# A mixture-of-experts encoder layer: the gather of all sorted tokens is issued behind the first pair's gate/up products instead of the second's

## The reference

```python
g_idx = argmax(g_logits)                       # 1 group of 4
top_w, top_i = lax.top_k(e_prob, TOP_K)        # 2 experts of its 8
for e in range(N_EXPERTS):                     # 32
    hg, hu = jnp.split(t @ w_gate_up[e], 2, axis=-1)
    out = out + comb[:, e:e + 1] * ((jax.nn.silu(hg) * hu) @ w_down[e])
x = layer_norm(DEEPNORM_ALPHA * x + out)
```

## Time and profile before

| | |
|---|---|
| Median of 3 runs | 496.63 us (495.29 to 497.02) |
| Profiled execution, its span | 494.7 us |
| Profiled execution, its own time | not given beside the span |
| PE busy / PEld busy | 472.1 us (95%) / 334.4 us (68%) |
| DVE, ACT, POOL busy | 244.9, 202.1, 222.8 us |
| DMA moved | 145.13 MB, mean 293 GB/s |

### The profile page before, as it was taken

The page is one execution under the profiler, slowest core; times in us unless marked ns, Lnnn a source line. Parts: engine busy times, 40 slices in busy tenths (PEclk is TensorE's granted clock), DMA queues, the critical chain, the costliest instruction groups (busy, mean ns, idle before and its releaser), DMA issues.

```text
span 494.7 us, 7686 instructions
## 1 busy us (share of the span) xinstructions
PE 472.1 (95%) x2816; PEld 334.4 (68%) x2816; DVE 244.9 (50%) x536; ACT 202.1 (41%) x447; POOL 222.8 (45%) x187
## 2 busy tenths in 40 slices
PE   8999999999999999999998999999999999998992
PEld 6999999898999999988973544444444444343441
DVE  1089999769996445630688242222222222122116
ACT  3544554489865696454542232222212212022112
POOL 3898999756765779998308011111111111011002
PEclk9999999999999999999998999999999999898997
DMA  8799985533533445559908979999999999999932
GB/s 289 256 364 346 362 295 171 197 103 128 172 127 129 141 159 171 177 181 380 422 32 318 390 291 425 421 421 421 421 421 422 420 420 423 421 421 421 420 154 86
DMA packets 26370, 145.13 MB, mean 293 GB/s; under 512 B 3040, under 2 KB 3296, under 8 KB 13792
## 3 DMA queue, kind: packets, MB, share of 16 engines
q1 hardware_dynamic: 26336, 144.67, 74.9%
HBM read 143.61 MB, written 1.05 MB: 292 GB/s over the span
## 4 chain that ended last, share of the span: by engine, by line
PE 86%; DVE 5%; ACT 3%; issue 2%; DMA 2%; SPq 1%; POOL 1%; DVEq 0%; ACTq 0%
PE bank L1474 21%; PE bank L1507 13%; PE bank L1226 12%; PE bank L1228 12%; PE bank L1227 12%; PE bank L1522 3%; PE bank L1523 3%; DMA raw<-in_w_in 2%; PE bank L1304 1%; PE bank L1282 1%; PE bank L1496 1%; DVE info L1113 1%; POOL w_lo L478 1%; PE bank L1448 1%; PE bank L1449 1%
## 5 line engine op out<-in xcount | busy, mean ns | idle before, releaser
L478 POOL TENSOR_TENSOR w_lo<-raw,w_hi 128x512 fp32r<-128x512 f32 x140 | 182.7, 1325 | 47.3 <-ACT w_hi L543 44.5
L543 ACT CAST w_hi<-raw 128x512 fp32r<-128x512 f32 x140 | 85.0, 619 | 80.7 <-PE bank L1228 71.1
L1226 PE MATMUL bank<-x_hi,w_hi 128*128 128x256 f32 x400 | 115.6, 289 | 1.4 <-POOL w_lo L478 1.4
L1228 PE MATMUL bank<-x_hi,w_lo 128*128 128x256 f32 x400 | 113.3, 283 | 0.0
L1227 PE MATMUL bank<-x_lo,w_hi 128*128 128x256 f32 x400 | 113.3, 283 | 0.0
L1474 PE MATMUL bank<-slots,raw 128*64 128x512 f32 x368 | 112.7, 593 | 0.0
L789 DVE SCALAR_TENSOR_TENSOR bank<-slots,par,bank 128x256 f32<-128x256 f32 x232 | 92.3, 482 | 0.2
L504 POOL COPY raw<-gates 128x512 f32 x28 | 19.8, 707 | 159.1 <-PE bank L1474 138.9
L1226 PEld LDWEIGHTS bank<-x_hi,w_hi 128*128 128x128 f32 x400 | 76.7, 192 | 2.1 <-issue 1.3
L1227 PEld LDWEIGHTS bank<-x_lo,w_hi 128*128 128x128 f32 x400 | 76.8, 192 | 0.3
L1228 PEld LDWEIGHTS bank<-x_hi,w_lo 128*128 128x128 f32 x400 | 76.8, 192 | 0.0
(11 more groups left out here) (211 smaller groups left out, 638.8 us busy)
## 6 DMA issues: line engine op xcount, KB each, us to landing
slots<-in_w_gate_up SPq DMA_DIRECT2D x46, 1024.0 KB, 15.6
slots<-in_w_down SPq DMA_DIRECT2D x32, 1024.0 KB, 16.4
raw<-in_w_in SPq DMA_DIRECT2D x48, 512.0 KB, 3.6
spare<-in_w_gate_up SPq DMA_DIRECT2D x10, 1024.0 KB, 16.1
late<-in_w_gate_up SPq DMA_DIRECT2D x8, 1024.0 KB, 20.0
raw<-in_w_attn SPq DMA_DIRECT2D x8, 512.0 KB, 3.2
raw<-in_w_conv SPq DMA_DIRECT2D x8, 512.0 KB, 3.2
raw<-in_w_out SPq DMA_DIRECT2D x8, 512.0 KB, 3.3
```

Of the source, the lines that this page charges most:

```text
L478: nc.gpsimd.tensor_tensor(w_lo[:, n % SPLIT, m], raw[:, b % RAW, m], w_hi[:, n % SPLIT, m].bitcast(F32), ALU.subtract).then_inc(w_lo_done, 1)
L543: nc.scalar.copy(w_hi[:, n % SPLIT, m], raw[:, b % RAW, m]).then_inc(w_hi_done, 1)
L1226: mm(dst, ah, bh, start=first, stop=False, **kw)
L1228: return mm(dst, al, bh, start=False, stop=last, **kw)
```

## The change

`gather_sorted` is called once, before the loop over the pairs and behind `gate_up(0, 0)` and `slot_info(0, 0)`, instead of in pair 1 behind its gate/up products. The chunks are taken in the order 4 to 7, 0 to 3. ScalarE and VectorE do `copy_sorted` in pair 0 instead of pair 1, behind `swish` and gate times up. Their wait for `pads_set` becomes a wait for `x1_set` ahead of the first chunk that lies over `ln_rows`. GpSimd clears the padding only when all chunks are copied. TensorE waits for `first_copied` ahead of the gather, and no longer for all copies behind it.

```diff
--- before.py
+++ after.py
@@ -108,6 +108,9 @@
 def last_tenant(e):
 
     return max((n for n in range(e) if GU_HOME[n] == GU_HOME[e]), default=None)
+
+
+SORTED_ORDER = [4, 5, 6, 7, 0, 1, 2, 3]
 
 
 C_IDENT, C_TRI, C_IOTA = 0, P, 2 * P
@@ -495,6 +498,8 @@
                 pool.wait_ge(x1_set, t + 1)
                 nc.gpsimd.tensor_tensor(xt[:, t, :], xt[:, t, :], ln_rows[:, 1, :], ALU.add).then_inc(x1_set, 1)
             pool.wait_ge(x1_set, 2 * TT)
+            pool.wait_ge(xgT_even, KT // 2)
+            pool.wait_ge(xgT_odd, KT // 2)
             nc.gpsimd.memset(xgT[:, :, ROUTED:], 0.0).then_inc(pads_set, 1)
 
             def take_tokens(u, first, second):
@@ -506,8 +511,6 @@
 
 
             pool.wait_ge(pads_set, 1)
-            pool.wait_ge(xgT_even, KT // 2)
-            pool.wait_ge(xgT_odd, KT // 2)
             with pool.Fori(1, PAIRS // 2) as i:
                 for u in range(2):
 
@@ -706,19 +709,20 @@
                     nc.scalar.copy(y_hi[:, c * HALF:(c + 1) * HALF], y_bank[c][:]).then_inc(y_hi_done, 1)
 
             def copy_sorted():
-                act.wait_ge(pads_set, 1)
-                for k in range(0, KT, 2):
-                    act.wait_ge(gathered, k + 1)
+                for i, k in enumerate(SORTED_ORDER[0::2]):
+                    if k == 0:
+                        act.wait_ge(x1_set, 2 * TT)
+                    act.wait_ge(gathered, 2 * i + 1)
                     nc.scalar.activation(xgT[:, k, 0:ROUTED], out_bank[k % 4][:], ACT.Identity, scale=ln1_gain(k),
                                          bias=ln1_shift(k)).then_inc(xgT_even, 1)
-                    if k >= 4:
-
-                        act.wait_ge(xgT_even, k // 2 + 1)
+                    if i >= 2:
+
+                        act.wait_ge(xgT_even, i + 1)
                         nc.scalar.mul(out_bank[k % 4][:], xt[:, k % 4 // 2, 0:HALF], ALPHA).then_inc(sums_by_act, 1)
 
             def pair(p, u, last=False):
                 swish(p)
-                if is_pair(p, 1):
+                if is_pair(p, 0):
                     copy_sorted()
                 copy_hT(p)
                 if not last:
@@ -1153,20 +1157,21 @@
                                             ALU.subtract).then_inc(y_lo_done, 1)
 
             def copy_sorted():
-                dve.wait_ge(pads_set, 1)
-                for k in range(1, KT, 2):
-                    dve.wait_ge(gathered, k + 1)
+                for i, k in enumerate(SORTED_ORDER[1::2]):
+                    if k == 1:
+                        dve.wait_ge(x1_set, 2 * TT)
+                    dve.wait_ge(gathered, 2 * i + 2)
                     nc.vector.tensor_scalar(xgT[:, k, 0:ROUTED], out_bank[k % 4][:], ln1_gain(k), ln1_shift(k),
                                             ALU.mult, ALU.add).then_inc(xgT_odd, 1)
-                    if k >= 4:
-
-                        dve.wait_ge(xgT_odd, k // 2 + 1)
+                    if i >= 2:
+
+                        dve.wait_ge(xgT_odd, i + 1)
                         nc.vector.tensor_scalar(out_bank[k % 4][:], xt[:, k % 4 // 2, HALF:], ALPHA, None,
                                                 ALU.mult).then_inc(sums_by_dve, 1)
 
             def pair(p, u, build=True):
                 gate_times_up(p, u)
-                if is_pair(p, 1):
+                if is_pair(p, 0):
                     copy_sorted()
                 build_scatter(p, u)
                 if build:
@@ -1439,10 +1444,11 @@
             def gather_sorted():
 
                 pe.wait_ge(compact_built, TT)
-                for k in range(KT):
-                    if k >= 4:
-
-                        pe.wait_ge(xgT_odd if k % 2 else xgT_even, (k - 4) // 2 + 1)
+                pe.wait_ge(first_copied, KT // 2)
+                for i, k in enumerate(SORTED_ORDER):
+                    if i >= 4:
+
+                        pe.wait_ge(xgT_odd if k % 2 else xgT_even, (i - 4) // 2 + 1)
                     n = slice(k * P, (k + 1) * P)
                     for t in range(TT):
                         mm(out_bank[k % 4][:], x1_hi[:, t, n], compact[:, t, :], start=(t == 0), stop=False)
@@ -1531,11 +1537,6 @@
 
                 if p >= 1:
                     gate_up(p, u)
-                    if p == 1:
-                        gather_sorted()
-
-                        pe.wait_ge(xgT_odd, KT // 2)
-                        pe.wait_ge(xgT_even, KT // 2)
                     scatter(p - 1, 1 - u, 0)
                 turn_h(p)
                 if p >= 1:
@@ -1549,6 +1550,7 @@
             gather_first()
             gate_up(0, 0)
             slot_info(0, 0)
+            gather_sorted()
             for p in range(PAIRS):
                 pair(p)
             for c in range(2):
```

## The result

The changed kernel took 497.55 us in the median of 20 runs (497.03 to 499.06), the kernel before 496.74 in 20 (494.91 to 498.21). The medians differ by 0.81 us, the means (496.44 and 497.98) by 1.54; the ratio is 1.0033, 95% interval 1.0023 to 1.0043, or 1.6 us, on the edge of what the prediction called no change. The forecast was 497.3, in a range of 495.0 to 499.6. The runs of both kernels fall into groups, which is why median and mean differ so: before 6 at 494.91 to 495.58, 13 at 496.41 to 497.17 and one at 498.21; after 11 at 497.03 to 497.59 and 9 at 498.51 to 499.06. The profiled execution took 498.8 us with a span of 496.7, against a span of 494.7 before.

A forecast was written before the change was run, and what follows sets the result against it. The prediction took the DMA queue's filling with expert weights as the bound: TensorE's 3.5 us gain becomes waits, landings move back 0.7 us, so 496.63 + 0.7 = 497.3 us, range 495.0 to 499.6.

The forecast's parts named there:

- TensorE's steps: First two pairs: forecast end times of TensorE's products, which set SP's issues; TensorE gains 3.5 us in all.
- the new wait: Ahead of the first pair's down products, TensorE waits about 1.2 us for ScalarE's copies; costs 0.8 us, clock stays up.
- the first issue wait: Pair 8's down products: TensorE, now earlier, first waits for down weights, near 377 us.
- the opposite view of the prediction: In the gather, each VectorE copy would wait out one of GpSimd's additions, 2.35 us; the prediction counted no hold.
- The mechanism: DMA queue: holes between issues set the end; the old 3.80 us hole goes, new ones of 3.2 and 1.9 to 2.5 us come.
- the hole at 292: DMA queue, 290 to 296 us in the kernel before: 3.80 us lost, forecast to go.
- The term of the DMA: DMA queue: every later landing moves back 0.5 to 1.1 us, or 0.3 to 0.9 measured alike; taken as +0.7 us.
- the pattern rival: Late pairs: large and small waits change places, pair 14's down products run at half clock, 1.7 us more: 499.0; chance 0.10.
- TensorE as the bound: Whole kernel: TensorE sets the end, so its 3.5 us gain reaches it: 493.1; chance 0.08.
- The clock rival: First pair's down products: the new wait lowers TensorE's clock, adding 1.7 us: 499.0; chance 0.18.
- The slowed gather: Gather: stopped by bank reuse or GpSimd slowed by copies, up to 1.6 us: 497.3 to 498.9; chance 0.08.

The follow-up runs named there:

- e2: Changed kernel with expert 9's gate/up load issued ahead of down 4 and 5 instead of behind down 6 and 7: 494.82 us.
- e3: Changed kernel with 12 filling products (result not used) on TensorE ahead of pair 2's down products: 497.91 us.
- e1b: Kernel before with 3 filling products (result not used) ahead of the first pair's turn and 1 ahead of its down products: 496.74 us.
- e8: Changed kernel with the first pair's turn mid-gather and ScalarE's copy of the turned hidden states ahead of chunk 0's: 496.82 us.
- e1: Kernel before with 7 filling products (result not used) ahead of the first pair's turn and 2 ahead of its down products: 497.44 us.
- e4b: Changed kernel with 3 filling products (result not used) in each of pairs 8 to 14, ahead of the wait for down weights: 497.49 us.
- e5: Changed kernel with the gather's chunks taken in the order 0 to 7: 501.75 us.
- e6: Changed kernel with the gather split: chunks 4 to 7 in the first pair, 0 to 3 behind the second pair's gate/up: 496.18 us.
- e7: e2 with 3 filling products (result not used) in each of pairs 10 to 14, ahead of the wait for down weights: 493.73 us.
- e9: Changed kernel with e2's load order, e8's turn and e7's filling products together: 492.5 us.

## Why the prediction was right, and where it was off

**TensorE's steps held.** Down 4 and 5 at 276.9 (276.72), gate/up 7 and 8 at 283.8 (283.58), down 6 and 7 at 289.9 (289.66); the new wait 1.2 us (1.38), without a fall of the clock; the first issue wait near 377 (376.62). TensorE gained its 3.5 us (3.75 by SP's issue of down 6 and 7) and they bought nothing. VectorE was not held by GpSimd: its copy at 265.91 took 0.81 us beside GpSimd's addition from 265.06 on, and 0.81 again at 271.36 behind the additions, by which the Trainium skill, "SBUF — State Buffer", section "Who interferes with whom", is borne out here for a copy that reads PSUM. Operations that read only SBUF fared otherwise, as the timelines before and after show:
```profile
265.56 2.03 DVE L1145 TENSOR_SCALAR w_lo<-con,kT 128x256 fp32r<-128x256 f32 x1
```
```profile
272.80 0.34 DVE L1149 TENSOR_SCALAR w_lo<-con,kT 128x256 fp32r<-128x256 f32 x1
```
Beside GpSimd's additions (before) it took 2.03 us, behind them (after) 0.34. For copies of that kind the opposite view of the prediction would have had weight.

**The mechanism held.** The gain of closing the hole at 292 is lost in two new ones. e2 shows it without touching TensorE, e3 shows that more work on TensorE in pair 2 is not what counts, and e1b and e8 confirm it from the other side: issues that came 1.65 and 1.40 us sooner brought pair 14 forward by 1.63 and 1.42. The holes were put at 3.2 and 1.9 to 2.5 us and measure 2.85 and 1.74.

**The term of the DMA was mis-sized.** It stood at +0.7 us, from holes of 5.1 to 5.7 us against 4.56. The holes measure 4.59: they are moved, not enlarged, by +0.03. Lost rose by 0.31 all the same, because the first 8 us of the queue cost 1.79 us in place of 1.50, a term that the prediction put at nothing. In the seven kernels with the whole gather in one piece in the first pair, SP's four issues of gate/up 5 and 6 take 2.60 to 3.19 us, in the other six 1.96 to 2.13, and in six of those seven the first 8 us lose more (1.79 to 2.49 us against 1.46 to 1.71; e2 has 1.52). Why, no run shows. Pair 14 moved by +0.36 us from the common issue, which is no more than before and e1 differ by.

**The time was hit in part by luck.** The forecast of 497.3 is 0.25 us from the median, but the means differ by 1.54 us and not by 0.7. By the groups of the runs this is made up so:

- The main groups moved by 0.51 us, 496.84 to 497.35. That is what the forecast speaks of.
- Nine of 20 runs lie 1.40 us higher, which adds 0.63 us to the mean. In the profiled one of them pair 14's down products ran at half clock, 1.7 us: the pattern rival, given 0.10 and wrongly argued against. That large and small waits alternate was taken for fixed; it is not. The 1.97 us wait at 449.64 lowered nothing, so the next pair had the long wait again, and the alternation shifted by one pair. It happens in other kernels too (e1, pair 14 at 5.35; e8, full clock behind 1.92 us). By their granted clocks it fits two more of the nine. The other six have the clock of the main group, as has the slower group of e4b, and a longer start of the kernel fits them (last section); that is argued and not shown.
- The kernel before also has fast runs, 6 of 20 at 494.91 to 495.58 and one at 498.21, which together take 0.40 us from its mean; the changed kernel has none so fast. Over all four sets of runs of the kernel before, 20 of 91 lie there. It is the time that e1b has when the first down products keep their clock, and the changed kernel has no such fall to escape. No profile of before in that state exists, so this too is argued only.

**The rivals.** TensorE as the bound fell: 5.4 us of added work moved pair 14 by 0.15 us, within what profiles of like kernels differ by (e3). The clock rival did not come about: 1.38 us of idle time left the clock at full. The slowed gather did not either: the gather's end and GpSimd's were as reckoned.

## What to carry to other kernels

Where a queue of loads sets the end, judge a move by the issues that it shifts and the holes between them (here that was right to about 1 us), not by the idle time that it fills on the busiest engine: 3.5 us gained on TensorE here were worth nothing, while one load taken forward to where its buffer comes free was worth 2.7 us with TensorE's program untouched. An engine with slack overall can still have single waits that cost their full length, namely those ahead of the instruction that frees a buffer. And before filling idle time, measure what one filling product takes.

## What the runs showed of the hardware

- Once the queue is full, weights come at 420 to 425 GB/s for over 150 us. From an issue into an empty queue to full rate pass 1.5 to 2.1 us (276.72 to about 278.7 in the changed kernel).
- A wait of 1.9 to 2.0 us lowers TensorE's clock only sometimes. In the changed kernel 1.92, 1.94 and 1.90 did and 1.97 did not. In nine profiles (before, after, e1, e1b, e2, e3, e5, e6, e8) the down products stand behind 27 waits of 1.88 to 2.19 us: 17 were followed by products of 5.32 to 5.35 us, 10 by 3.65, among them the wait of 2.15 (e3). In pairs 8 to 14 no wait of 0.94 us or less lowered it, nor did 1.38 us in the first pair; 1.72 and 0.43 us shortly one after the other did (before, first pair).
- VectorE's `w_lo` took 2.03 us beside GpSimd's additions and 0.34 behind them, its next operation (`gat`) 2.57 and 0.42; its copies out of PSUM took 0.81 in both places.
- The first 32 products of the kernel take 7.17 to 7.55 us in ten profiles and 9.2 to 9.3 in three (e3, e5, e6), with a granted clock of 1.00 shown in both, though in 8 to 10 us only 6 products run, against 11 before and after. Everything behind stands 1.5 us later then, which is why the table counts from a common issue, and may be why runs of one kernel fall into groups some 1.5 us apart. The profiled runs fit: with the long start they lie high among the runs of their kernel (e5: 503.06, where three took 501.64 to 501.75), and those of e1b, e2, e4b, e7, e8 and e9, with a short start and pair 14 at full clock, lie in the lowest group. But no kernel was profiled with both starts, so it is not shown. From the timelines of e6 and of the kernel before:
```profile
6.55 9.29 PE L1253 MATMUL bank<-gates,raw 128*128 128x256 f32 x32 [0.62 <-DMA raw<-in_w_in]
```
```profile
6.65 7.17 PE L1248 MATMUL bank<-gates,raw 128*128 128x256 f32 x32 [1.12 <-DMA raw<-in_w_in]
```
